# RWKV-7 chunks on one core: odd heads' token-side operands on the other half of the partitions

## What is computed

```python
def step(S, inp):
    r_t, w_t, k_t, a_t, b_t, v_t = inp
    sa = jnp.einsum('bhvk,bhk->bhv', S, a_t)
    S = S * w_t[:, :, None, :] + sa[..., None] * b_t[:, :, None, :] + v_t[..., None] * k_t[:, :, None, :]
    return S, jnp.einsum('bhvk,bhk->bhv', S, r_t)
```

## Time and profile before

| | us |
|---|---|
| median of three runs | 997.94 (997.13 to 998.85) |
| the profiled execution | 996.85 |
| its span, first to last instruction | 995.1 |
| TensorE busy | 879.6 (88%) |
| VectorE busy | 561.5 (56%) |
| ScalarE busy | 333.3 (33%) |
| GpSimd busy | 147.6 (15%) |

### The profile page before, as it was taken

The page is one execution under the profiler, slowest core; times in us unless marked ns, Lnnn a source line. Parts: engine busy times, 40 slices in busy tenths (PEclk is TensorE's granted clock), DMA queues, the critical chain, the costliest instruction groups (busy, mean ns, idle before and its releaser), DMA issues.

```text
span 995.1 us, 21494 instructions
## 1 busy us (share of the span) xinstructions
PE 879.6 (88%) x8900; PEld 541.4 (54%) x8900; DVE 561.5 (56%) x933; ACT 333.3 (33%) x585; POOL 147.6 (15%) x296
## 2 busy tenths in 40 slices
PE   2799999996999998667888888899996699999996
PEld 0445445564655554466777777754575344444442
DVE  1524016778768696865566566587316244555457
ACT  3221110141113636665665664312310122223223
POOL 6000111103000010432234322000001000100041
PEclk9899999997999979789999999999975799999998
DMA  9810422212224400112211122591008679999957
GB/s 331 326 52 1 161 107 96 67 67 101 85 85 170 154 16 1 35 21 48 43 35 30 33 40 64 172 328 78 22 22 285 221 258 369 370 366 371 343 127 228
DMA packets 119760, 142.46 MB, mean 143 GB/s; under 512 B 49964, under 2 KB 85224, under 8 KB 119272
## 3 DMA queue, kind: packets, MB, share of 16 engines
q1 hardware_dynamic: 110824, 116.55, 35.7%
q0 software_dynamic: 3744, 13.63, 4.4%
q10 hardware_dynamic: 5088, 10.82, 2.8%
HBM read 122.99 MB, written 18.00 MB: 142 GB/s over the span
## 4 chain that ended last, share of the span: by engine, by line
PE 82%; DVE 5%; issue 4%; ACT 4%; DMA 3%; POOL 1%; SPq 1%; ACTq 0%; DVEq 0%; POOLq 0%
PE bank L1937 74%; PE bank L1941 8%; ACT region L931 2%; DMA region<-in_w_ada_dram 2%; DMA rk_r<-h_rows_dram,slot_tokens 1%; DMA region<-in_w_in_dram 1%; POOL yg_b L832 1%; DVE cl_b L1855 1%; DVE region L1926 0%; ACT ada_row_buffers L931 0%; ACT w_sb L931 0%; DVE region L1340 0%; DVE region L1922 0%; ACT vtok_b L931 0%; DVE region L1908 0%
## 5 line engine op out<-in xcount | busy, mean ns | idle before, releaser
L1937 PE MATMUL bank<-region 64*64 64x64 f32 (+3 forms) x3904 | 401.9, 299 | 30.8 <-DVE region L1535 9.5
L1937 PEld LDWEIGHTS bank<-region 64*64 64x64 f32 (+1 forms) x3904 | 233.1, 149 | 186.0 <-issue 160.8
L931 ACT ACTIVATE region<-bank 128x256 f32<-128x256 f32 (+3 forms) x216 | 98.0, 454 | 369.5 <-PE bank L1937 271.2
L1941 PE MATMUL bank<-ident,region 128*128 128x128 f32 (+2 forms) x403 | 67.7, 303 | 28.5 <-DMA scratch<-in_gla_gk_dram 12.7
L1937 PE MATMUL bank<-region,rk_r 128*128 128x512 f32 x176 | 79.9, 608 | 0.8 <-issue 0.8
L1941 PEld LDWEIGHTS bank<-ident,region 128*128 128x128 f32 (+2 forms) x403 | 50.1, 155 | 44.9 <-issue 35.3
L1907 DVE TENSOR_SCALAR region<-region 128x256 f32<-128x256 f32 x16 | 4.7, 294 | 100.2 <-ACT region L931 100.2
L1396 DVE SCALAR_TENSOR_TENSOR rk_r<-region,vec,rk_r 128x512 f32<-128x512 f32 x64 | 49.2, 768 | 12.3 <-ACT rk_r L931 10.2
L1937 PEld LDWEIGHTS bank<-region,rk_r 128*128 128x128 f32 x176 | 33.5, 196 | 39.6 <-issue 38.4
L906 POOL DMA_INDIRECT rk_r<-h_rows_dram,slot_tokens x16 | 15.2, 951 | 247.2 <-PE bank L1941 131.7
L1578 DVE TENSOR_TENSOR region<-bank,region 128x256 f32<-128x256 f32 x60 | 25.5, 425 | 41.1 <-PE bank L1937 39.9
(11 more groups left out here) (277 smaller groups left out, 1159.3 us busy)
## 6 DMA issues: line engine op xcount, KB each, us to landing
region<-in_moe_w_dram SPq DMA_DIRECT2D x38, 1024.0 KB, 10.1
region<-in_w_ada_dram SPq DMA_DIRECT2D x12, 2048.0 KB, 8.5
region<-in_w_in_dram SPq DMA_DIRECT2D x6, 2048.0 KB, 8.0
cl_b<-in_moe_w_dram SPq DMA_DIRECT2D x10, 1024.0 KB, 12.8
expert_rows_dram<-yg_b ACTq DMA_DIRECT2D x14, 512.0 KB, 6.9
region<-late_condition_dram SPq DMA_DIRECT2D x3, 1024.0 KB, 9.4
a_rows_dram<-region SPq DMA_DIRECT2D x20, 128.0 KB, 2.8
region<-inverse_rows_dram SPq DMA_DIRECT2D x20, 128.0 KB, 3.0
```

Source lines behind the costliest of these rows:

```text
L931: return act.activation(out, in_, func, **kw)
L1937: return pe.matmul(out, lhsT, rhs, start=start, stop=stop)
L1941: return pe.transpose(out, in_, ident[0:n, 0:n])
```

## The change

Odd heads' token-side operands go to the other half: half(cp ^ hp) in place of half(cp). So even heads use tiles (0,0) and (1,1) in AV, WU and Y, odd heads (0,1) and (1,0). Even heads' results go to one bank, odd heads' to another.

To lay the operands so, the transposes of b, k and v (tB, tK, vt) become 16 products of 64x64 with a 64x64 identity (`crossed`), into two banks, with two ScalarE copies of 128x256 in place of one of 128x512. AV gets two banks. WU keeps two, but by parity in place of by head number, and both are counted filled at the end. The list of jobs for a round is then k k WU WU tK tK b b Z8 Z8 X8t G G tB tB tA X16 X16 Z16 Z16 seq seq X16t Y Y X32 X32 AV AV X32t Z32 Z32 L L X64 X64 (36 jobs, 8 banks as before).

The values are wanted uncrossed by `head_norm` after the loop: SyncE stores the odd heads' values with their halves exchanged to `v_dram` (two DMAs of 128 x 20 pieces of 256 bytes in all, at H = 0) and loads them back for each tile (five DMAs, `uncross`: tile 0 at H = 4, tiles 2 and 3 at H = 8, tile 4 ahead of the loads of w_out, tile 1 after the last Y). `head_norm` waits for them.

```diff
-            jobs += inside(s, pair("k", s)) + inside(H, pair("WU", H))
-            jobs += inside(s, [("tK", s)] + pair("b", s) + pair("Z8", s) + [("X8t", s)]) + ...
+            jobs += inside(s, pair("tK", s) + pair("b", s) + pair("Z8", s) + [("X8t", s)]) + ...
+            jobs += inside(s, pair("tB", s) + [("tA", s)] + pair("X16", s) + pair("Z16", s)) + ...
+            jobs += inside(s, pair("X32", s) + pair("AV", s) + [("X32t", s)] + pair("Z32", s)) + ...
+            def crossed(n, h, srcs):
+                bs = [open_bank(n, h, 0), open_early(n, h, 1)]
+                for i in range(RC):
+                    for cp in range(2):
+                        for hp in range(2):
+                            last = mm(bs[hp][half(cp ^ hp), i * HD:(i + 1) * HD], srcs[i][half(hp), half(cp)], ident[half(hp), half(hp)])
 def scored_v(h):
-                for n in range(NH):
-                    for cp in range(2):
-                        ins = mm(b[half(cp), n * HD:(n + 1) * HD], g.K2[half(cp), 0, n], vtok[half(cp), t, n * HD:(n + 1) * HD])
+                for i in range(RC):
+                    for cp in range(2):
+                        for hp in range(2):
+                            n, mine = 2 * i + hp, half(cp ^ hp)
+                            last = mm(bs[hp][half(cp), i * HD:(i + 1) * HD], g.K2[mine, 0, n], vtok[mine, t, n * HD:(n + 1) * HD])
 def wu_rows(h):
-                    for n in range(4 * j, 4 * j + 4):
-                        for cp in range(2):
-                            ins = mm(b[half(cp), (n % 4) * 2 * HD:(n % 4 + 1) * 2 * HD], g.XB[half(cp), n], g.X[half(cp), n])
+                            last = mm(bs[hp][half(cp ^ hp), i * 2 * HD:(i + 1) * 2 * HD], g.XB[half(cp), n], g.X[half(cp), n])
 def rows_from_chunk(h):
-                        mm(o, g.B[half(cp), 0, n], g.WU[half(cp), n, HD:2 * HD], n < 2, False)
-                        ins = mm(o, g.K2[half(cp), 1, n], vtok[half(cp), t, n * HD:(n + 1) * HD], False, False)
+                        mine = half(cp ^ n % 2)
+                        mm(o, g.B[mine, 0, n], g.WU[mine, n, HD:2 * HD], n < 2, False)
+                        ins = mm(o, g.K2[mine, 1, n], vtok[mine, t, n * HD:(n + 1) * HD], False, False)
 def head_norm(n):
+                dve.wait_ge(s_vnat, (16, 48, 48, 64, 80)[n])
```

More of the change, by code:

```diff
@@ L345, in trunk_program @@
         jobs += unit("v1") + [("L", 0, 0), ("L", 0, 1)] + unit("v2") + unit("v3") + [("bonus",), ("L", 1, 0), ("L", 1, 1)]
-        jobs += [("vt", t) for t in range(NT)]
+        jobs += [("vt", t, hp) for t in range(NT) for hp in range(2)]
         NS = 2 * NT
@@ L358, in trunk_program @@
             jobs += inside(s, pair("k", s)) + inside(H, pair("WU", H))
-            jobs += inside(s, [("tK", s)] + pair("b", s) + pair("Z8", s) + [("X8t", s)]) + inside(H, pair("G", H)) + last(H, "G")
-            jobs += inside(s, [("tB", s), ("tA", s)] + pair("X16", s) + pair("Z16", s)) + inside(H, [("seq", H, 0)])
+            jobs += inside(s, pair("tK", s) + pair("b", s) + pair("Z8", s) + [("X8t", s)]) + inside(H, pair("G", H)) + last(H, "G")
+            jobs += inside(s, pair("tB", s) + [("tA", s)] + pair("X16", s) + pair("Z16", s)) + inside(H, [("seq", H, 0)])
             jobs += inside(H if H < NS - 2 else -1, [("seq", H, 1)]) + inside(s, [("X16t", s)]) + inside(H, pair("Y", H))
@@ L363, in trunk_program @@
                 jobs += [("st", 0), ("st", 1), ("s0",), ("mrow",)]
-            jobs += inside(s, pair("X32", s) + [("AV", s), ("X32t", s)] + pair("Z32", s)) + inside(l, pair("L", l)) + inside(s, pair("X64", s)) + last(s, "X64")
+            jobs += inside(s, pair("X32", s) + pair("AV", s) + [("X32t", s)] + pair("Z32", s)) + inside(l, pair("L", l)) + inside(s, pair("X64", s)) + last(s, "X64")
         for n in range(NT):
@@ L2302, in state_from_chunk @@
                 p, d, g, t = step(h)
-                wait_result(pe, "tK", h)
+                for hp in range(2):
+                    wait_result(pe, "tK", h, hp)
                 ks = range(2 if h < NS - 2 else 1)
```

102 lines of the change are left out of this document (73 added, 29 removed).

## The result

The changed kernel takes 1007.83 us in the median (1005.5 to 1012.27), the kernel before 997.54 on the same chip (995.64 to 998.85): a ratio of 1.0109, 95% interval 1.0076 to 1.0142. It is slower by about 10 us, where 4.8 us less were forecast. The profiled execution took 1005.5 us with a span of 1003.7 us, 8.6 us more than the span before.

The account below looks back on a forecast made before the run. TensorE's own work was taken as the bound (82% of the chain). Gains of 4.8 us in eight rounds, 0.4 in round 1 and 0.6 in round 9, less 0.5 and 0.5, gave 4.8: median 993.1 us, 80% range 988.5 to 998.5.

Parts of the forecast that it names:

- WU worth nothing, Z8 0.18 us later: In each loop round, WU's 0.85 us saving gains nothing; Z8 waits for `masked_k` and starts 0.18 us later.
- Ahead of the loop, 0.5 us: Turning the values by products before the loop loses 0.5 us, with bounds of 0.1 and 1.5.
- AV covered by VectorE: AV's saving of about 0.4 us a round is worth nothing, since X32t behind it waits for VectorE's X32 sum.
- Y, 0.78 us a round gained: Y's products on four tiles save 0.78 us on the path, so X16t, its copy and X32 come earlier.
- Transposes as products, zero: For tB and tK, products cost 0.55 us against 0.52 to 0.59 for four transposes; taken as zero, at most 0.1 either way.
- The stream of instructions, 0 to 3 us, 0.5 taken: TensorE's 1,400 added instructions, together with the values' DMAs, cost between 0 and 3 us; 0.5 taken.
- A sign with a slip: Sign in the changed trace: three rounds of the loop take 61.0 us in place of 62.3.
- A: Rival, 7%: WU's gain comes through as well, 0.85 + 0.18 us more in each of eight rounds, 984.9 us.
- B: Rival, 21%: Y's gain is taken back by a slower rate or the inverse's DMAs ahead of Z8; 996.7 or 997.0 us.
- C: Rival, 12%: TensorE's clock falls in the new 1.0 us gap ahead of Z8; nine rounds cost 15 us, 1008.

## Why the prediction was wrong

**WU worth nothing, Z8 0.18 us later: right.** The gap of 1.09 us ahead of Z8, ended by `masked_k`, is the one forecast. Ending it gave about 3 us in the run with tK late, 0.3 us in each of nine rounds, where 0.18 was forecast.

**Ahead of the loop, 0.5 us: right.** It is 5.87 us from the first of the values' products to the loop's first product, against 5.41.

**AV covered by VectorE: right in kind.** X32t waits for the X32 sum after as before; L1605 ends 3.2 us of idle time in six rounds.

**Y, 0.78 us a round gained: wrong.** The four-tile rate was reached. But the products use instructions at 9 ns each, and in the round shown the gap inside Y is larger than the gain. With the rate taken away again, work rose by 6.6 us and "issue" fell by 5.4.

**Transposes as products, zero: the step that failed.** The array time was right to 0.03 us a set. The price was asked of the array alone; the two sets took 16 slow instructions out of a round and put 128 fast ones in, and with the values' products ahead of the loop those alone made the kernel 11.6 us slower.

**The stream of instructions, 0 to 3 us, 0.5 taken: the term of the sum that was mis-sized.** It measured 12.1 us of "issue" in six rounds, and 16.9 us more of gaps at a block's start. I had bounded it by how much the stream grows, 1,400 of 17,800, and by the one long gap. Growth was the wrong measure. The evidence was in the trace of before: 14 of 47 packets had a gap of over 0.4 us behind them, and the 10 of these at a block's start lay behind denser stretches than the block starts without one (1.48 against 1.94 us for 108 instructions).

**A sign with a slip.** By its own sum, three rounds at 0.6 less are 60.5 us, not 61.0. It changes nothing here: three rounds take some 65.7 us after.

**Rivals.** A did not come. B had a part of the sign and the wrong place: Y's gain was taken back, but no slower rate did it, and a DMA of the inverse ended one gap only in the whole loop, 1.24 us ahead of the Z8 at 451.20, where before 2.55 us stood. The Trainium skill's rule on row groups ("TensorE: Matmul & The Clock Gate", The mechanism), which had a share in B, shows nowhere: the rates of four tiles were reached. C's time, 1008, is almost the measured one, and that is luck: three falls more than before in the stretch, up to 4.8 us, where C had nine. They do not stand in the gap ahead of Z8, once a round, as C had it; two of the five stand behind gaps from the supply, and the products for transposes alone lose as much without one fall more. The Trainium skill's rule on the evacuation of PSUM ("TensorEngine Tiling (Array Packing)", PSUM Bottleneck) agrees with the 5.0 us more of waits for results, the smaller part of what came.

**What stays open**: how the 10 us divide between gaps, clock and waits for results in the median, since profiles of equal loops differ by some 4 us of "issue"; why the fetch starts as late as it does; and why products of 64x128 were slower still. That a slower supply would cost more, or a faster one return the gain, could not be tried: no kernel sets it.

## What to carry to other kernels

When TensorE's products are small, price an edit in instructions and in nanoseconds per instruction as well as in array time: before believing a gain, look for idle time that "issue" ended, and whether it follows the packets of the instruction queue. Where it does, faster products only reach the gap sooner, and slow transposes or two-tile products between them are the time in which the next block arrives. A quick look at places helps: gaps that recur at one remainder of the instruction's number by 256 belong to the stream. A transpose is one matmul and one weight load; the same turn by 64x64 f32 products is eight times as many.

## What the runs showed of the hardware

- Three gaps at a block's start, of 1.98 us before and of 1.81 and 1.56 us after, were followed by falls of the granted clock to 1.2 GHz, one of 1.72 us was not; the fall worked out cost 1.7 us of full speed. The other falls followed waits for results or a mixture.
- TensorE's instructions came in packets of 16,384 bytes, one for 257 instructions by the count of packets; 30 of 35 gaps behind one stood at one place of 256, and stayed at it when 64 instructions were put ahead. A gap ended 2.48 us after the packet's start, and 108 instructions had been left at the start (medians). In the changed kernel's six rounds the gaps at a block's start lasted 0.86 us (median of 21); with the sets at 33 ns an instruction "issue" was back at 6.2 us.
- Half transposes (64 rows by 128) of both halves of the partitions into two banks took 0.39 us for eight, where four of 128x128 took 0.59. A MATMUL with a stationary operand of 64x128 took 65 ns, those of 64x64 took 17 on four tiles and 29 on two.
- ScalarE can copy 64 partitions of a bank to the other 64, three copies of 256 columns in 1.21 us, the last two of them by halves (ScalarE's timeline of the kernel with crossing by copies):

```profile
560.19 1.21 ACT L955 ACTIVATE region<-bank 128x256 f32<-128x256 f32 x3
```
